# One more seven-product pair at the start of feed-forward blocks 2 and 3, and the norms' inverse roots by Ln and Exp on ScalarE

## What is computed

```python
def rms_norm(x, gain):
    xf = x.astype(jnp.float32)
    y = xf * lax.rsqrt(jnp.mean(xf * xf, axis=-1, keepdims=True) + RMS_EPS)
    return (y * gain.astype(jnp.float32)).astype(x.dtype)

def swiglu(x, w_gate, w_up, w_down):
    return (jax.nn.silu(x @ w_gate) * (x @ w_up)) @ w_down

# in each layer, g = norm_gains[layer]
x = x + FFN_RESIDUAL * swiglu(rms_norm(x, g[0]), ffn_w_gate[layer, 0], ffn_w_up[layer, 0], ffn_w_down[layer, 0])
# x = x + the layer's mixer of rms_norm(x, g[1])
x = x + FFN_RESIDUAL * swiglu(rms_norm(x, g[2]), ffn_w_gate[layer, 1], ffn_w_up[layer, 1], ffn_w_down[layer, 1])
```

## Time and profile before

| what | value |
|---|---|
| median of three runs | 1955.03 us |
| profiled execution | 1955.77 us |
| its span | 1954.0 us |
| TensorE (PE) busy | 1948.1 us, 100% |
| VectorE (DVE) busy | 1397.9 us, 72% |
| ScalarE (ACT) busy | 851.6 us, 44% |
| GpSimd (POOL) busy | 527.3 us, 27% |
| DMA | 265.92 MB, mean 136 GB/s |

### The profile page before, as it was taken

The page is one execution under the profiler, slowest core; times in us unless marked ns, Lnnn a source line. Parts: engine busy times, 40 slices in busy tenths (PEclk is TensorE's granted clock), DMA queues, the critical chain, the costliest instruction groups (busy, mean ns, idle before and its releaser), DMA issues.

```text
span 1954.0 us, 28996 instructions
## 1 busy us (share of the span) xinstructions
PE 1948.1 (100%) x11722; PEld 1707.3 (87%) x11722; DVE 1397.9 (72%) x1882; ACT 851.6 (44%) x1230; POOL 527.3 (27%) x394
## 2 busy tenths in 40 slices
PE   9999999999999999999999999999999999999999
PEld 7999998877789999988999998877777888999997
DVE  7877776554588877768877776773458657877773
ACT  6443333535554344345433444442546345333431
POOL 1322222142223322223322322200015413322221
PEclk9999999999999999999999999999999999999999
DMA  6556663351346666545666653232200235666653
GB/s 211 155 164 171 173 168 95 119 181 55 88 126 176 174 172 167 147 129 145 178 166 172 181 151 114 97 96 88 76 1 1 87 116 160 177 173 168 178 141 107
DMA packets 112469, 265.92 MB, mean 136 GB/s; under 512 B 10321, under 2 KB 22865, under 8 KB 112337
## 3 DMA queue, kind: packets, MB, share of 16 engines
q1 hardware_dynamic: 92336, 225.72, 35.3%
q0 software_dynamic: 19856, 38.28, 12.5%
q10 hardware_dynamic: 144, 0.09, 0.0%
HBM read 259.32 MB, written 4.72 MB: 135 GB/s over the span
## 4 chain that ended last, share of the span: by engine, by line
PE 98%; DVE 1%; DMA 0%; issue 0%; ACT 0%; SPq 0%; POOL 0%; DVEq 0%
PE BANKS L656 12%; PE BANKS L658 12%; PE BANKS L657 12%; PE BANKS L579 11%; PE BANKS L580 11%; PE BANKS L581 11%; PE BANKS L709 6%; PE BANKS L710 6%; PE BANKS L711 6%; PE BANKS L1022 2%; PE BANKS L850 1%; PE BANKS L852 1%; PE BANKS L851 1%; PE BANKS L999 1%; PE BANKS L1005 1%; PE BANKS L813 1%
## 5 line engine op out<-in xcount | busy, mean ns | idle before, releaser
L656 PE MATMUL BANKS<-BF,ASH 128*128 128x256 f32 x876 | 248.0, 283 | 0.0
L658 PE MATMUL BANKS<-BF,ASL 128*128 128x256 f32 x876 | 247.9, 283 | 0.0
L657 PE MATMUL BANKS<-BFL,ASH 128*128 128x256 f32 x876 | 247.9, 283 | 0.0
L579 PE MATMUL BANKS<-XH,HI 128*128 128x512 f32 x624 | 245.7, 394 | 0.7 <-DVE XL L1593 0.3
L1657 DVE TENSOR_TENSOR LO<-RING,HI 128x1024 fp32r<-128x1024 f32 (+2 forms) x204 | 216.3, 1060 | 41.2 <-ACT HI L1160 39.9
L580 PE MATMUL BANKS<-XL,HI 128*128 128x512 f32 x624 | 243.2, 390 | 0.0
L581 PE MATMUL BANKS<-XH,LO 128*128 128x512 f32 x624 | 243.0, 389 | 0.0
L1173 ACT ACTIVATE TMP<-TMP 128x512 f32<-128x512 f32 x88 | 55.7, 633 | 406.4 <-DVE TMP L1686 406.4
L2262 POOL TENSOR_TENSOR TMP<-TMP,RSTD 128x512 f32<-128x512 f32 x88 | 132.0, 1499 | 365.3 <-ACT TMP L1173 365.3
L2254 POOL DMA_DIRECT2D ASR<-gu_dram x73 | 88.1, 1219 | 387.5 <-DMA ASR<-gu_dram 381.5
L709 PE MATMUL BANKS<-HH,DHI 128*128 128x512 f32 x488 | 190.7, 391 | 0.0
(11 more groups left out here) (249 smaller groups left out, 4875.5 us busy)
## 6 DMA issues: line engine op xcount, KB each, us to landing
RING<-gu_dram SPq DMA_DIRECT2D x174, 512.0 KB, 3.9
ASR<-gu_dram SPq DMA_DIRECT2D x146, 256.0 KB, 2.9
ASR<-gu_dram POOLq DMA_DIRECT2D x73, 512.0 KB, 6.9
DRAW<-down_dram SPq DMA_DIRECT2D x40, 512.0 KB, 3.7
RING<-oin_dram SPq DMA_DIRECT2D x32, 512.0 KB, 3.5
RING<-down_dram SPq DMA_DIRECT2D x32, 384.0 KB, 3.2
DRAW<-down_dram SPq DMA_DIRECT2D x24, 384.0 KB, 3.7
RING<-ein_dram SPq DMA_DIRECT2D x16, 512.0 KB, 3.6
```

The lines of the kernel that those rows point to most:

```text
L579: pe.matmul(PS[bank][:], HI[j][:, c], hi(k), start=(n == 0), stop=False)
L656: pe.matmul(out, w_hi[:, c], x_hi(k), start=(k == 0), stop=False)
L657: pe.matmul(out, w_hi[:, c], x_lo(k), start=False, stop=False)
L658: last = pe.matmul(out, w_lo[:, c], x_hi(k), start=False, stop=(k == 3))
```

## The change

Blocks 2 and 3 get two plain pairs instead of three, so pair 2 becomes a Strassen pair. The pieces of the down product keep their places (`EARLY_FROM` has the old numbers). The work that prepares and finishes pair 2 is put into the orders of all engines, with some steps moved: `form_split(f, 3)` now stands ahead of the norm, `split(4)` behind the sums, `up(0)` behind the split of the sums, and the sums of pair 3 ahead of `up(1)`, the last plain up tile. In `block` the wait for the pair's banks moves from the first product to the third (five). In all blocks and in the odd mixer the inverse root is Ln and then Exp(-0.5 x) on ScalarE, and VectorE's reciprocal goes. TensorE now waits for the finished inverse root (`rstd_ready`) where it waited for the root.

```diff
-PLAIN = (5, 4, 3, 3)
+PLAIN = (5, 4, 2, 2)
+EARLY_FROM = (5, 4, 3, 3)
...
@@ tensor, block(p)
                     pe.wait_ge(lo_ready, n + 1)
-                    pe.wait_ge(bank_free, n + 2)
+                    if f < 2:
+                        pe.wait_ge(bank_free, n + 2)
                     if p == PLAIN[f]:
-                        pe.wait_ge(std_ready, r + 1)
+                        pe.wait_ge(rstd_ready, r + 1)
...
                     product(PS[4][:, low], *summed(p, 0), form(1)).then_inc(seven_done, 1)
+                    if f >= 2:
+                        pe.wait_ge(bank_free, n + 2)
                     product(gate_bank[:, high], *summed(p, 1), form(0)).then_inc(five_done, 1)
...
@@ scalar, norm(r)
-                act.activation(RSTD[:], AUX[:], ACT.Sqrt, scale=1.0 / DM, bias=EPST[:]).then_inc(std_ready, 1)
+                link(act.activation(RSTD[:], AUX[:], ACT.Ln, scale=1.0 / DM, bias=EPST[:]))
+                act.activation(RSTD[:], RSTD[:], ACT.Exp, scale=-0.5).then_inc(rstd_ready, 1)
@@ scalar, block_ffn
                     form_inputs(f, 3)
+                    form_split(f, 3)
                     norm(now)
-                    split(4, whole)
-                    form_split(f, 3)
+                    split(2 * first, whole)
+                    sums_split(first, 0)
+                    sums_split(first, 1)
                     silu(0, 1.0)
-                    split(5, whole)
-                    sums_split(first, 0)
+                    split(2 * first + 1, right)
                     h_high(0)
-                    silu(1, 1.0)
-                    split(2 * first, whole)
-                    h_high(1)
...
                     copy_one(p)
-                    if p == first:
+                    ahead = f >= 2 and p == first
+                    if ahead:
+                        split(2 * nxt, whole)
+                        sums_split(nxt, 0)
+                        sums_split(nxt, 1)
+                    if not has_early(f, p - 1):
                         h_high(p - 1)
...
@@ scalar, root(h) of the odd mixer
-                        act.activation(RSTD[:], RSTD[:], ACT.Sqrt).then_inc(tstd_ready, 1)
+                        link(act.activation(RSTD[:], RSTD[:], ACT.Ln))
+                        act.activation(RSTD[:], RSTD[:], ACT.Exp, scale=-0.5).then_inc(factor_root, 1)
@@ vector, norm(r)
-                dve.wait_ge(std_ready, r + 1)
-                dve.reciprocal(RSTD[:], RSTD[:]).then_inc(rstd_ready, 1)
                 dve.wait_ge(rstd_ready, r + 1)
@@ vector, block_ffn
                     form(f, 3)
+                    form_split(f, 3)
                     norm(now)
-                    split(4, whole)
                     gate(0)
-                    form_split(f, 3)
-                    up(0)
-                    split(5, whole)
-                    gate(1)
                     sums_second(first)
                     sums_third(first)
-                    up(1)
                 dve.wait_ge(sum_made, 2 * block_count(f, first) + 2)
                 split(2 * first, whole)
                 sums_split(first, 0)
                 sums_split(first, 1)
+                if f >= 2:
+                    up(0)
                 gate(first - 1)
                 split(2 * first + 1, right)
+                if f >= 2:
+                    sums_second(first + 1)
+                    sums_third(first + 1)
                 up(first - 1)
```

More of the change, by code:

```diff
@@ L311, in trunk @@
         vh_ready, pth_ready, ptl_ready = sem("vh_ready"), sem("pth_ready"), sem("ptl_ready")
[L312 to L313 removed]
+        num_done, den_abs, num_sq, ssq_step, factor_root, num_read = (
+            sem(n) for n in ("num_done", "den_abs", "num_sq", "ssq_step", "factor_root", "num_read"))
         column_sum, factor_ready, den_ready = sem("column_sum"), sem("factor_ready"), sem("den_ready")
@@ L383, in leads @@
         def leads(f, p):
-            return has_early(f, p) and (p == PLAIN[f] or not has_early(f, p - 1))
+            return has_early(f, p) and not has_early(f, p - 1)
         def early_pairs(f):
@@ L461, in block_ffn @@
                     p = n // 2 - 1
-                    if n == plain + 1:
+                    if n == plain + 1 and has_early(f, PLAIN[f]):
                         load_early(PLAIN[f])
-                    elif n % 2 and p == ALONE[f]:
+                    elif n % 2 and p >= PLAIN[f] and leads(f, p + 1):
                         load_early(p + 1)
@@ L1268, in block_ffn @@
                     copy_one(p)
-                    if p == first:
+                    ahead = f >= 2 and p == first
[4 more added lines that the diff above has]
+                    if not has_early(f, p - 1):
                         h_high(p - 1)
+                    if p == first and has_early(f, p):
                         early_split(p)
-                    elif not has_early(f, p - 1):
-                        h_high(p - 1)
-                    if nxt:
+                    if ahead:
+                        split(2 * nxt + 1, right)
+                    elif nxt:
                         split(2 * nxt, whole)
@@ L1853, in block_ffn @@
                     elif nxt:
-                        sums_second(nxt)
-                        sums_third(nxt)
+                        if p == first:
+                            mid_two(p)
+                            mid_five(p)
+                            mid_three(p)
+                        else:
+                            sums_second(nxt)
+                            sums_third(nxt)
                         dve.wait_ge(sum_made, 2 * block_count(f, nxt) + 2)
                         split(2 * nxt, whole)
-                        mid_two(p)
-                        mid_five(p)
-                        mid_three(p)
+                        if p > first:
+                            mid_two(p)
+                            mid_five(p)
+                            mid_three(p)
                         sums_split(nxt, 0)
@@ L2087, in head_factor, with root_ready @@
                                              ALU.add).then_inc(factor_ready, 1)
-                def invert_factor(h):
-                    dve.wait_ge(tstd_ready, h + 1)
-                    link(dve.reciprocal(RSTD[:], RSTD[:]))
+                def root_ready(h):
+                    dve.wait_ge(factor_root, h + 1)
                 def scale_numerator(h, c):
```

23 lines of the change are left out of this document (11 added, 12 removed).

## The result

| | before | after |
|---|---|---|
| median of 13 runs | 1954.99 us (1954.57 to 1955.52) | 1959.55 us (1959.22 to 1960.42) |
| profiled execution | 1955.77 us | 1959.52 us |
| its span | 1954.0 us | 1957.8 us |

The changed kernel is 4.6 us slower: ratio 1.0024 [1.0016, 1.0031]. The forecast was 1956.8 us, between 1953.2 and 1959.2.

A forecast was written before the change was run, and what follows sets the result against it. TensorE, busy 1948.1 of 1954.0 us, was taken as the bound. Block 2's +2.4 and block 3's -0.6 gave +1.8 us on the profiled 1955.77, 1957.6; less 0.74 for the median, 1956.8 us, range 1953.2 to 1959.2.

The forecast's parts named there:

- The saving: Blocks 2 and 3: a Strassen pair takes 10.07 us against a plain pair's 10.88, saving 0.81 us each.
- Inverse root in block 2: Start of block 2: split, two table loads, Ln and Exp give RSTD at 900.1, 1.7 us later than before.
- the third rival: Table switches on ScalarE hold it for longer than the load, as long again (1.28 us): 1963.0 us; 3%.
- First product: Block 2, pair 2: TensorE starts at 903.6 where 902.35 was due, 1.2 us late.
- Third product: Block 2, pair 2: waits for `up(0)` to read bank 1, starts at 907.55, 1.1 us late.
- Pair 3: Block 2: sums beside GpSimd delay it; loses 0.4 (no overlap) to 1.4 us (full), taken as 0.9.
- Block 3: Start of block 3: pair 2 has time to spare, 0.2 us lost; net -0.6 us, between -0.8 and -0.5.
- The second rival: Block 3 stalls as block 2 does, unit 4 landing 1.9 us later: +4.5 us, 1959.5 us; 11%.
- The odd mixer: V's high part behind the root is the one tight place: 0 to 0.3 us in three heads, taken as 0.
- The signs of being wrong: Block 2: Exp ends before 899, or pair 2 starts within 0.3 us of 902.35; odd mixer grows over a microsecond.
- the second sign: Start of block 2: Exp ending before 899, against a forecast end near 900.1, would show the forecast wrong.
- The first rival: Block 2 starts as block 3 does, the gaps don't arise and both savings stay: 1953.4 us; 27%.

The follow-up runs named there:

- block3_ordered: Kernel after with three plain pairs kept in block 2, old root in the odd mixer's heads, Silu, `up(0)` and copies reordered in block 3: 1954.76 us, ratio 0.9997.
- old_root: Kernel after with Sqrt and the reciprocal again in the odd mixer's four heads: 1959.08 us, ratio 1.0021 to the kernel before.

## Why the prediction was wrong

The mechanism was right in block 2: pair 2's inputs come late, TensorE waits where I said, for what I said, and the saving is outweighed. One wait there I hadn't named: 0.55 us at the second product of pair 3, for the split of its sums (ASL). In block 3, which was to keep most of its saving, and in the odd mixer, which was to lose nothing, the forecast had no loss of this kind. What failed is the size of three terms: the overlap with GpSimd in pair 3 of block 2, `copy_one(3)` in block 3, and the odd mixer, taken at nothing. By the traces they make up 1.05, 0.67 and 0.89 of the 3.0 us between +1.8 and +4.8; the other 0.4 are small losses in block 2, mostly behind the waits, which the sum left out.

- **The saving**, 0.81 us a pair: right. block3_ordered stands at -0.80 behind its pair 3.
- **Inverse root in block 2**, Exp's end at 900.1: right. The program ran 1.04 us early there, and Exp ended at 898.41 + 0.63 = 899.04. ScalarE in the kernel after, from the form's split, beside the earlier trace rows:

```profile
894.03 1.06 ACT L1146 ACTIVATE BF<-BFR 128x1024 fp32r<-128x1024 f32 x1 [2.32 <-DVE BFR L1643]
895.11 1.28 ACT L1127 ACT_TABLE_LOAD   x1
896.41 0.69 ACT L1127 ACTIVATE RSTD<-BANKS,EPST 128x512 f32<-128x512 f32 x1
897.11 1.28 ACT L1128 ACT_TABLE_LOAD   x1
898.41 0.63 ACT L1128 ACTIVATE RSTD<-RSTD 128x512 f32<-128x512 f32 x1
```

  Ln takes 0.69 and Exp 0.63, as taken. Between two dependent activations a table switch costs its load and no more (897.11 + 1.28 = 898.39, Exp at 898.41), so the third rival falls. The drain that the Trainium skill puts behind a load (ScalarE: Activation LUTs, What ACT_TABLE_LOAD costs) isn't in these rows.
- **First product**, 1.2 us: measured 1.09, and 0.1 behind the restart. Right.
- **Third product**, 1.1 us: measured 1.16 and 0.1. Right, but for the restart, which I had left out at each wait. At the fourth and the seventh product of pair 2 another 0.1 and 0.15 were lost, so that the two products and `copy_one(2)` together are at 1.09 + 1.60 = 2.69 where I had 2.35.
- **Pair 3**, 0.9 us between 0.4 and 1.4: measured 1.95, and the largest error. I had the second sum at 1.67, the first at 1.2 instead of 0.69, and left open whether unit 6's split meets GpSimd. Measured are 1.79, 1.67 and 2.32 for the split of the sums behind them; unit 6's split is alone (1.22), because GpSimd is the one that waits for it. The row of 1.67 showed the price. What I didn't see in it is the rule: whoever comes second waits until the other has finished. By it, both sums would have been at full price, since h's low part and the next product stand back to back on GpSimd at that time, and one of the two splits too.
- **Block 3**, -0.6 us between -0.8 and -0.5: measured +0.07. The first two products are in time, as worked out, with RSTD at 1625.28 + 0.63 = 1625.91 (1622.2 and the 3.7 us that the program is late there). The whole loss is `copy_one(3)`, for which I took 0.2 us; it is 0.88 by the trace. By the rows its cause is that of pair 3 in block 2, the two sums beside GpSimd; no run has GpSimd's operations small in block 3. VectorE in block 3 after:

```profile
1634.49 1.78 DVE L1673 TENSOR_TENSOR ASR<-ASR,RING 128x512 f32<-128x512 f32 x1
1636.31 1.68 DVE L1679 TENSOR_TENSOR ASR<-ASR,RING 128x512 f32<-128x512 f32 x1
```

  The second rival, a late landing of unit 4, gave nearly the measured time (1959.5), but for another reason: no wait for `up(0)` stands in block 3.
- **The odd mixer**, 0: measured +0.89, of which old_root takes away 0.7. The step that failed is "the one tight place is V's high part". In the rows of heads 1 and 2 the tight place is the path from the root through the weights' exponent (0.5 us later) and GpSimd's y_low to VectorE's reads of the banks.
- **The signs of being wrong.** One of the three came up by its letter: pair 2 of block 2 starts at 902.40, within 0.3 us of 902.35. That sign was given as a time of day, and the program ran 1.04 us early there, so it says nothing here: against the 901.31 at which it was due the pair is 1.09 us late. For the same reason Exp, at 899.04, only just misses the second sign, an end before 899. A sign given as a distance from the matmul ahead would have held.
- **The first rival**, that the gaps don't arise: wrong in block 2, and in block 3 true only in part, with `copy_one` moved.

How the waits hang together wasn't predicted at all. Each new order took away the wait that it aimed at, and a later one took up much of its time: 0.24 us came from a removed wait of 0.9, 0.5 from another of 1.0. What VectorE is behind has to be made good somewhere, and here it is made good only at pair 4. Not tried: moving GpSimd's two operations so that they lie beside VectorE's reads of banks, which by these rows might cost neither engine anything, and another order of mids and sums in pair 4.

## What to carry to other kernels

When a change packs operations of VectorE closely behind each other, lay GpSimd's timeline beside them: in these traces operations of both engines with two SBUF inputs take turns, so a pair that overlaps costs the sum of both. A wait that moves a value on one engine moves everything queued behind it; look at each instruction there, not only at the one with a name in the diff. And where several chains are tight at once, removing the wait that shows gains only as much as the next one leaves.

## What was new about the hardware

- VectorE (two SBUF inputs, 128x512) beside GpSimd: 1.67 to 1.79 us where 0.68 alone; 128x1024: 2.32 where 1.22 alone; with one input in a PSUM bank 0.68 either way.
- GpSimd is held up in the same way: 2.32 us where 1.29 is the shortest.
- A matmul of 256 tokens behind a wait of TensorE is drawn 0.39 us long where 0.28 is usual, and the next starts some 0.1 us later. The four waits of block 2 after are 3.35 us by their rows and cost 4.4.
- The compiler's load of a function table costs 1.28 us and nothing behind it. It put one between Ln and Exp at all six norms and all four heads after.
